# Two transformer blocks in one kernel: modulation sums folded with block transposes, residual additions moved in GpSimd's queue

## The reference

```python
mods = silu(c) @ w_ada + b_ada          # w_ada: 2048 x 12288, six rows of 2048
mods_c = silu(c_ctx) @ w_ada + b_ada    # the context needs the first two only
h = rms_norm(x) * g * (1 + scale) + shift
x = x + gate_a * (mix(h, hc) @ w_out)   # four kinds of attention, 16 heads
x = x + gate_f * ffn(rms_norm(x) ...)
out = rms_norm(x) * g_final
```

## Time and profile before

| | us |
|---|---|
| median of 3 runs (2425.19 to 2425.72) | 2425.29 |
| the profiled execution | 2426.32 |
| its span, first to last instruction | 2424.6 |
| TensorE products busy | 2402.5 |
| TensorE weight loads busy | 1977.9 |
| VectorE busy | 1800.6 |
| ScalarE busy | 1119.0 |
| GpSimd busy | 162.2 |

### The profile page before, as it was taken

How to read it: one execution, slowest core, us unless ns; L and a number is a source line. 1 busy time by engine, 2 the same in 40 slices (tenths; PEclk the granted TensorE clock), 3 DMA queues, 4 the chain that set the end, 5 groups by cost and what they waited for, 6 DMA issues and landing times.

```text
span 2424.6 us, 28710 instructions
## 1 busy us (share of the span) xinstructions
PE 2402.5 (99%) x11098; PEld 1977.9 (82%) x11098; DVE 1800.6 (74%) x2429; ACT 1119.0 (46%) x1464; POOL 162.2 (7%) x186
## 2 busy tenths in 40 slices
PE   9999999999999999999999999999999999999998
PEld 7888888888888888888788888777788888888887
DVE  5688868888899888788878857677777765555555
ACT  5344444444455454456743333644544443444443
POOL 2010000000000001000011100002000100000000
PEclk9999999999999999999999999999999999999999
DMA  9888766666588668877985656455898976667663
GB/s 303 256 269 273 239 218 195 195 184 195 188 267 267 211 213 292 293 257 255 316 270 186 222 171 233 132 159 177 268 302 283 292 233 193 195 211 227 210 213 124
DMA packets 280100, 556.93 MB, mean 230 GB/s; under 512 B 18503, under 2 KB 23901, under 8 KB 278428
## 3 DMA queue, kind: packets, MB, share of 16 engines
q1 hardware_dynamic: 270588, 515.16, 66.0%
q0 software_dynamic: 9088, 37.85, 5.4%
q10 hardware_dynamic: 288, 2.10, 0.2%
HBM read 543.07 MB, written 15.11 MB: 230 GB/s over the span
## 4 chain that ended last, share of the span: by engine, by line
PE 94%; DVE 3%; issue 1%; ACT 1%; DMA 1%; SPq 0%; POOL 0%; ACTq 0%; POOLq 0%; DVEq 0%
PE pb L2155 92%; PE pb L2159 3%; DVE wlo L1395 1%; DMA raw<-in_w_in 1%; DVE acc L1417 1%; ACT whi L939 0%; DVE sm L1946 0%; DVE x L1774 0%; DVE across L1427 0%; DVE gn L2015 0%; DVE x L1777 0%; DVE x L1495 0%; DVE stz L1497 0%; DVE x L1510 0%; DVE fl L2003 0%
## 5 line engine op out<-in xcount | busy, mean ns | idle before, releaser
L939 ACT ACTIVATE whi<-raw 128x1024 fp32r<-128x1024 f32 (+1 forms) x791 | 828.2, 1049 | 1105.5 <-PE pb L2155 1030.5
L1395 DVE TENSOR_TENSOR wlo<-raw,whi 128x1024 fp32r<-128x1024 f32 (+1 forms) x791 | 958.1, 1218 | 446.8 <-ACT whi L939 444.6
L2155 PE MATMUL pb<-whi,xh 128*128 128x512 f32 (+1 forms) x1184 | 465.1, 393 | 0.7 <-DVE xl L1548 0.7
L2155 PE MATMUL pb<-whi,xl 128*128 128x512 f32 (+1 forms) x1184 | 458.2, 387 | 0.0
L2155 PE MATMUL pb<-wlo,xh 128*128 128x512 f32 (+1 forms) x1184 | 457.6, 386 | 0.0
L1417 DVE SCALAR_TENSOR_TENSOR acc<-raw,silc,acc 128x512 f32<-128x512 f32 x480 | 346.1, 752 | 5.7 <-DMA raw<-in_w_ada 0.7
L2155 PE MATMUL pb<-whi,fh 128*128 128x512 f32 x704 | 274.8, 390 | 1.4 <-DVE fl L2003 1.4
L2155 PE MATMUL pb<-whi,fl 128*128 128x512 f32 x704 | 274.0, 389 | 0.0
L2155 PE MATMUL pb<-wlo,fh 128*128 128x512 f32 x704 | 273.9, 389 | 0.0
L2155 PEld LDWEIGHTS pb<-whi,xh 128*128 128x128 f32 x1184 | 222.6, 188 | 46.6 <-issue 2.9
L2155 PEld LDWEIGHTS pb<-whi,xl 128*128 128x128 f32 x1184 | 222.3, 188 | 46.0
(11 more groups left out here) (426 smaller groups left out, 2828.9 us busy)
## 6 DMA issues: line engine op xcount, KB each, us to landing
raw<-in_w_in SPq DMA_DIRECT2D x375, 512.0 KB, 4.6
raw<-in_w_ada SPq DMA_DIRECT2D x192, 512.0 KB, 4.9
raw<-in_ffn_wg SPq DMA_DIRECT2D x88, 512.0 KB, 4.4
raw<-in_ffn_wu SPq DMA_DIRECT2D x88, 512.0 KB, 4.8
raw<-in_ffn_wd SPq DMA_DIRECT2D x88, 512.0 KB, 4.1
raw<-in_w_branch SPq DMA_DIRECT2D x64, 512.0 KB, 3.9
raw<-in_w_out SPq DMA_DIRECT2D x64, 512.0 KB, 4.4
scr_h<-sil POOLq DMA_DIRECT2D x11, 512.0 KB, 4.0
```

The lines of the kernel that those rows point to most:

```text
L939: return eng.activation(dst, src, ACT.Copy)
L1395: tt(wlo[:, u, a:b, 0:n], raw[:, l % NRAW, a:b, 0:n], f32(whi[:, u, a:b, 0:n]), ALU.subtract) \
L2155: return eng.matmul(dst, l, r, start=start, stop=stop)
```

## The change

- Each result in `acc` (32 of them) is folded on VectorE alone, in the chain `fold`, which stands near the end of its list and has step `ada_beat[p] + 1 + m`. One block transpose in place turns every 32 x 32 block of `acc`; one reduction over runs of 32 leaves 16 columns in `part`, 128 x 256. What remains is a sum over the four groups of 32 partitions.
- TensorE makes that sum with a table `kfold` (the 32 x 32 identity repeated four by four): one product of 256 columns for pieces 0 to 7, and one of 64 columns for each four of the others, five in all. VectorE adds the bias while it takes the result, four additions on 32 partitions each.
- A piece waits for the fold of the one that used its half of `acc`. `across`, the copies, GpSimd's `fold` and the transposes are gone. `kfold` is loaded in GpSimd's chain `tables`.
- GpSimd's residual additions of quarters 0 to 2 of token block 1 have steps 502, 506 and 510, ahead of the load of `x2` for token block 0. The fourth of token block 1 follows that load directly, and the four of token block 0 follow in steps 515 to 521. There is now one semaphore per token block.

```diff
         co, si = np.cos(ang), np.sin(ang)
         return np.stack([np.concatenate([co, co], -1), np.concatenate([-si, si], -1)], 1).astype(np.float32)
 
+    c["k_fold"] = np.tile(np.eye(32, dtype=np.float32), (4, 4))
     c["k_rope128"] = rope(128)
     c["k_rope64"] = rope(64)
     return c
...
         ident = small("ident", [128, 128])
         par = small("par", [128, 112])
         mod = small("mod", [128, 8, 16])
-        across = small("across", [128, 512])
+        part = small("part", [128, 256])
+        kfold = small("kfold", [128, 128])
         bcol = small("bcol", [128, 96])
         rope_off = small_at[0]
         ropeA = small("ropeA", [128, 2, 2, 128])
...
 
 
 
-        pairs = [[(p, 0), (p, 1)] for p in range(8)] + [[(p, 0), (p + 1, 0)] for p in range(8, len(pieces), 2)]
-        pair_of_piece = {p: f for f, pair in enumerate(pairs) for p, _ in pair}
+        groups = [range(8)] + [range(p, p + 4) for p in range(8, len(pieces), 4)]
+
+        def part_of(p, m):
+            rows, n = pieces[p][1], pieces[p][2]
+            return 16 * (4 * rows[m] + n if p < 8 else p - 8)
 
         def sub_done(i):
             s, _, _, end = subs[i]
...
         B["h2"] = E["o3"], E["o3"] + 2
         B["gT"] = [ada_beat[11] + 9, ada_beat[23] + 9]
         B["gta"] = B["ot"][7] + 2
+        B["ada"] = [ada_beat[g[-1]] + 6 for g in groups]
+        B["ada"][3] = ada_beat[19] + 5
         B["hid"] = [E[f"fu{s}"] for s in range(11)]
 
         GAP = dict(na=5, gq=4, ml=3)
...
                               scr_row.rearrange("h x -> (h x)").partition_broadcast(128)) \
                     .then_inc(*M.inc(S("scr_band"), "scr_band", by=16))
 
-            def fold():
-                for f, pair in enumerate(pairs):
-                    yield from until(ada_beat[pair[1][0]] + 1)
-                    W.wait_ge("across", f, 2)
-                    eng.tensor_tensor(acc[:, 1, :], acc[:, 1, :], across[:, :], ALU.add) \
-                        .then_inc(*M.inc(S("folds"), "fold", f))
-
             def ln_rows(key, b, k, g, bias):
                 yield from until(b)
                 W.wait_ge("exb_free", k - 1)
...
                 eng.dma_start(ropeB[:, :, :, :].rearrange("p t a b -> p t (a b)"),
                               I["k_rope64"].rearrange("(t p) a b -> p t (a b)", p=128)) \
                     .then_inc(*M.inc(S("rope_in"), "rope", by=16))
+                eng.dma_start(kfold[:, :], I["k_fold"]).then_inc(*M.inc(S("kfold_in"), "kfold", by=16))
                 for i, n in enumerate(("gqa_gq_2", "gqa_gk_2", "diff_gsub_2")):
                     eng.dma_start(grow[:, i, :], I[n][0].partition_broadcast(128)) \
                         .then_inc(*M.inc(S("grow_in"), "grow", i, by=16))
...
                 W.wait_ge("acc", "dfv", 3)
                 W.wait_ge("scr_x1", 1)
                 eng.dma_start(x2[:, 1, :], scr_x1[:, 1, :]).then_inc(*M.inc(S("x2_in1"), "x2", 1, by=16))
+
+                def add(n, tb):
+                    W.wait_ge("x2", tb)
+                    W.wait_ge("ev", f"p{n}", tb)
+                    d = x2[:, tb, n * 512:(n + 1) * 512]
+                    eng.tensor_tensor(d, d, x2p[:, tb, n * 512:(n + 1) * 512], ALU.add) \
+                        .then_inc(*M.inc(S(f"x2_sum{tb}"), "x2p", n, tb))
+
+                for n in range(3):
+                    yield from until(E[f"p{n}"] + 5)
+                    add(n, 1)
                 yield from until(E["o0"])
                 W.wait_ge("pv", "ml", 3)
                 eng.dma_start(x2[:, 0, :], scr_x1[:, 0, :]).then_inc(*M.inc(S("x2_in0"), "x2", 0, by=16))
+                add(3, 1)
                 for n in range(4):
-                    for tb in (1, 0):
-                        W.wait_ge("x2", tb)
-                        W.wait_ge("ev", f"p{n}", tb)
-                        d = x2[:, tb, n * 512:(n + 1) * 512]
-                        eng.tensor_tensor(d, d, x2p[:, tb, n * 512:(n + 1) * 512], ALU.add) \
-                            .then_inc(*M.inc(S("x2_sum"), "x2p", n, tb))
+                    yield from until(E["o0"] + 2 + 2 * n)
+                    add(n, 0)
 
             def gates():
                 for r in range(2):
...
                             .then_inc(*M.inc(S("hs_in"), "hs", s, a, by=16))
 
             chains = [start(), na_table(), band_table(), ln_rows("ln_b", B["ln_b"], 1, "sgu_ln_g", "sgu_ln_b"),
-                      ln_rows("ln_d", B["ln_d"], 3, "conv_ln_g", "conv_ln_b"), tables(), attention1(), residual(), fold(),
+                      ln_rows("ln_d", B["ln_d"], 3, "conv_ln_g", "conv_ln_b"), tables(), attention1(), residual(),
                       context(), norm1(), gqa(), mla1(), out2(), gates(), norm2(), hidden(), final(), na_bias(), diff()]
             for i in range(NSUB + 2):
                 beat[0] = i
...
                 W.wait_ge("raw", l)
                 if x == 0:
                     W.wait_ge("silc")
-                    if pair_of_piece[p]:
-                        W.wait_ge("across", pair_of_piece[p] - 1, 2)
-                        if 1 in slots[p]:
-                            W.wait_ge("ada_sum", pair_of_piece[p] - 1)
+                    for m in range(two):
+                        if 0 < p < 8:
+                            W.wait_ge("folded", p - 1, m)
+                        elif p >= 8:
+                            W.wait_ge("folded", *((7, p - 8) if p < 10 else (p - 2, 0)))
                     if p == 0:
                         W.wait_ge("relT")
                 for k in range(2):
...
                             ins = stt(a, raw[:, l % NRAW, k, :], c, a, ALU.mult, ALU.add)
                         ins.then_inc(*M.inc(S("ada_acc"), "ada", p, x + k, m))
                 M.value["raw_free", l] = M.value["ada", p, x + 1, two - 1]
-                f = pair_of_piece[p]
-                if x == 14 and p == pairs[f][1][0]:
-                    if f:
-                        W.wait_ge("fold", f - 1)
-                    for h in range(2):
-                        q, m = pairs[f][h]
-                        W.wait_ge("ada", q, 15, m)
-                        eng.tensor_copy(across[64 * h:64 * h + 64, :], acc[64 - 64 * h:128 - 64 * h, h, :]) \
-                            .then_inc(*M.inc(S("across"), "across", f, h))
-                    W.wait_ge("across", f, 1)
-                    eng.tensor_copy(acc[0:64, 1, :], acc[0:64, 0, :]).then_inc(*M.inc(S("across"), "across", f, 2))
-
-            def ada_end(f):
-                yield from until(sum_beat[f] + 1)
-                (p, _), (p1, m1) = pairs[f]
-                col, (r0, r1, n) = pieces[p][0] // 128, (pieces[p][1][0], pieces[p1][1][m1], pieces[p][2])
-                W.wait_ge("ada_sum", f)
-                sums = side("ada_sum", f)[:, :].rearrange("p (q h t) -> p q h t", q=4, h=2)
-                if r0 == r1:
-                    dst = mod[:, r0, 4 * n:4 * n + 8]
-                    eng.tensor_reduce(dst.rearrange("p (h q) -> p q h", h=2), sums, AX, ALU.add) \
-                        .then_inc(*M.inc(S("mod_sum"), "mods", f))
-                    W.wait_ge("mods", f)
-                    tt(dst, dst, bcol[:, col:col + 8], ALU.add).then_inc(*M.inc(S("mod"), "mod", r0, n))
-                    M.value["mod", r0, n + 1] = M.value["mod", r0, n]
-                else:
-                    eng.tensor_reduce(mod[:, r0:r1 + 1:r1 - r0, 4 * n:4 * n + 4].rearrange("p h q -> p q h"), sums, AX,
-                                      ALU.add).then_inc(*M.inc(S("mod_sum"), "mods", f))
-                    W.wait_ge("mods", f)
-                    for r in (r0, r1):
-                        dst = mod[:, r, 4 * n:4 * n + 4]
-                        tt(dst, dst, bcol[:, col:col + 4], ALU.add).then_inc(*M.inc(S("mod"), "mod", r, n))
+
+            def fold():
+                for p in range(len(pieces)):
+                    for m in range(len(pieces[p][1])):
+                        yield from until(ada_beat[p] + 1 + m)
+                        a, k = acc[:, slots[p][m], :], part_of(p, m)
+                        W.wait_ge("ada", p, 15, m)
+                        eng.transpose(a, a).then_inc(*M.inc(S("ada_t"), "turned", p, m))
+                        W.wait_ge("turned", p, m)
+                        if p == 8:
+                            W.wait_ge("ada_sum", 0)
+                        eng.tensor_reduce(part[:, k:k + 16], a.rearrange("p (j r) -> p j r", r=32), AX, ALU.add) \
+                            .then_inc(*M.inc(S("ada_fold"), "folded", p, m))
+
+            def ada_end(g):
+                yield from until(sum_beat[g] + 1)
+                W.wait_ge("ada_sum", g)
+                for a in range(4):
+                    q = slice(32 * a, 32 * a + 32)
+                    if g == 0:
+                        sums = side("ada_sum", g)[q, 0:256].rearrange("p (t c m a) -> p t c m a", t=2, c=2, m=16)
+                        bias = bcol[q, 0:32].rearrange("p (c m) -> p c m", c=2).unsqueeze(1).broadcast_to([32, 2, 2, 16])
```

(31 more changed lines are left out.)

## The result

The changed kernel takes 2415.14 us at the median of five runs (2414.43 to 2415.77) against 2425.19 for the kernel before on the same chip: ratio 0.9958, 95% interval 0.9945 to 0.9972. That is faster, by 10.1 us or 0.4%; the forecast was 2414.7 us, and its range holds the time. The span of the profiled execution went from 2424.6 to 2414.0 us.

A forecast was written before the change was run, and what follows sets the result against it. TensorE's products bound the kernel, busy 2402.5 of 2424.6 us. From the profiled 2426.3: less 7.3 (transposes), plus 1.4 (products), less 4.7 (stall) gives 2415.7; less 1.0 offset, 2414.7 us; range 2412.5 to 2419.6.

The forecast's parts named there:

- Transposes out, products in: TensorE's queue: 16 sums by transposes leave (7.3 us by starts), five products with `kfold` enter (1.4 us), net 5.9 us.
- rival of durations: A transpose on TensorE is worth its recorded duration: 17.5 us out, about 3 in, time 2406; chance 0.03.
- The stall: TensorE's wait near 1661 us, costing 5.5 us with lost clock: 0.8 us stays, clock holds, gain 4.7 us.
- The spread: GpSimd's residual additions 0 to 2 of token block 1 run before the hold, costing VectorE nothing on the path.
- rival of a spread that does not take place: All eight additions still run behind GpSimd's hold; about 2418 us; chance 0.16 together with the full stall.
- VectorE elsewhere: VectorE outside the stall: about 36 us out, 44 plus some 3 in, 11 us more work, hidden by its four-step lead.
- Slower: Folds ahead of `wlo` make TensorE wait where VectorE is full; 2437 us if half of 44 us came through; chance 0.04.

The follow-up runs named there:

- products_x10: The changed kernel with each of the five products with `kfold` made ten times into the same bank; 2427.54 us.
- transposes_x5: The kernel before with the four transposes of each of its 16 sums made five times; 2451.32 us.
- adds_only: The kernel before with its old modulation sums, but GpSimd's residual additions spread as in the change; 2422.78 us, ratio 0.9987.
- sums_only: The new modulation sums with the residual additions in their old order, eight behind the hold; 2416.72 us, ratio 0.9966.
- fold_x3: The changed kernel with each block transpose of VectorE's folds made three times in a row; 2422.35 us.

## Why the prediction was right

- **Transposes out, products in.** Forecast 7.3 less 1.4; by the starts above 7.3 less 1.35 (0.43 + 4 x 0.23). Right, and `products_x10` and `transposes_x5` rule out the rival of durations: 11.6 to 12.4 and 25.3 us instead of 26.5 and 70. The products' busy time fell by 8.0 us and not by about 6; the 1.7 us of clock at the stall are busy time too, which would explain it. The 275 ns of the Trainium skill, page "TensorE: Matmul & The Clock Gate", section "Part 4: PE-mode transpose", are the length of the record; as a price in a full stream the trace has 0.11 us.
- **The stall.** Forecast: 0.8 us stay and the clock holds, a gain of 4.7. Measured, in the forecast's own frame (start against due time): 1.0, with 0.84 of it idle, clock 1.00, gain 4.4. The steps held but for one: transpose and reduction took 0.70 and 0.69 us against 0.69 each, while the evacuations took 3.0 us instead of 2.7, because GpSimd's four additions took 1.73 us each instead of 1.61 and still reached into the first L1520 (1.07 us). The forecast was also too firm: this wait depends on a phase of 0.05 us between two engines, and a second execution had no idle piece. That the profiled execution had the slow phase, as the kernel before had, is luck.
- **The spread.** Three additions ran early at no cost to TensorE, as forecast: `adds_only` loses nothing against the kernel before until the stall. `sums_only` and `adds_only` show that the halves overlap: 9.6 and 4.1 us of span alone, 10.6 together. The rival of a spread that does not take place falls.
- **VectorE elsewhere.** Forecast 11 us more work; its busy time rose by 0.6 us. The terms themselves held (44.4 us for the 32 folds, 3.6 for the small additions), but the low parts alone came out 5.5 us shorter (L1404 has 952.6 us of busy time; it had 958.1 over the same 791). Most of this is delay under GpSimd's 16 additions of `acc`, which the account had left out: in the trace of the kernel before, seven low parts that overlap one of them are 4.4 us longer together than undisturbed ones. It lay beside TensorE.
- **Slower.** The rival's mechanism exists (`fold_x3`), but at the folds' true size the waits where VectorE is full are no longer than before (1.22 and 0.64 us against 1.46 and 0.64). The two rules of the Trainium skill, page "VectorE: DVE Perf Modes", section "Rules for kernel authors", that the prediction set against the change did not bite (transpose 128 x 128 on TensorE; `tensor_reduce` is the slowest operation): the fold turns blocks of 32 x 32 and never needs a whole 128 x 128 transpose, and the reduction took 0.69 us, no more than an addition of the same size.
- **What was missed.** The prediction says that SP's queue keeps its order and counts what GpSimd's table load delays, but not what the removed waits in GpSimd's queue had delayed. That cost up to 0.75 us of idle time near 955 us, 1.0 by starts in the first execution. The sum is right in spite of it partly by luck, since waits at 1111 and 1159 us came out 0.6 us shorter and the first 12 us 0.2 shorter.

## What to carry to other kernels

Price an instruction on the bound engine by the distance of starts before and behind it, not by its record, and a wait likewise: one with 0.84 us of idle time cost 1.1. When a waiting instruction is taken out of a queue, ask what stands behind it: its wait may have been the only thing that spread out large loads. And when two edits both relieve one stall, count it once.

## What was not expected of the hardware

- A VectorE operation on two SBUF operands and a GpSimd one exclude each other so strictly that 0.05 us of order decides over 1.1 us (2.35 against 3.45 us for the same two VectorE operations).
- Seven loads of 5 MB issued at once raise the median landing time of 512 KB loads from 6 or 7 us to between 8 and 15, at 400 GB/s, for some 20 us.
- Waits of TensorE of 0.84, 1.12, 1.56 and 1.60 us, and 1.46 with 0.64 behind it, left the granted clock at 1.00. It fell to half (1.2 GHz) behind waits of 0.53 and 2.04 us five microseconds apart, behind 2.45 and 1.03, and behind 3.03.
